# The first four weight units of three narrow stages read x before its norm, and the norm's factor is put on afterwards

## The reference, cut to what matters

```python
def rms_norm(x, g):
    y = xf * lax.rsqrt(jnp.mean(xf * xf, axis=-1, keepdims=True) + RMS_EPS)
    return (y * g.astype(jnp.float32)).astype(x.dtype)
def mod_norm(x, m, i, g):
    return rms_norm(x, g) * (1 + m[:, 3 * i + 1, None]) + m[:, 3 * i, None]
def swiglu(h, w1, w2):
    a, b = jnp.split(h @ w1, 2, axis=-1)
    return (jax.nn.silu(a) * b) @ w2
...
        h = mod_norm(x, m, 1, norm_g[l, 1])
        u = h @ w_in[l]
        if last:
            uc_kv = hc @ w_in[l][:, OFF_K:]
```

## Time and profile before

| | us |
|---|---|
| median of 3 executions | 2800.92 (2800.55 to 2805.89) |
| profiled execution, its own time | 2799.17 |
| span of the profiled execution | 2797.3 |
| TensorE busy | 2732.1 (98%) |
| VectorE busy | 2067.0 (74%) |

### The profile page before, as it was taken

One profiled execution on the slowest core, in us unless ns is written; L12 is line 12 of the kernel. 1 busy time (PEld: TensorE's weight loads), 2 busy tenths in 40 slices (PEclk: granted clock), 3 DMA queues, 4 the chain that ended last, 5 costly groups with the idle time before them and its releaser, 6 DMA issues.

```text
span 2797.3 us, 40204 instructions
## 1 busy us (share of the span) xinstructions
PE 2732.1 (98%) x15618; PEld 2320.2 (83%) x15618; DVE 2067.0 (74%) x3773; ACT 1216.9 (44%) x2228; POOL 522.2 (19%) x449
## 2 busy tenths in 40 slices
PE   7999999999999999999988999999999999999998
PEld 5888878668888878888885999889999888888887
DVE  6989895568989896564766766765896677777776
ACT  5323233453232342222445545565556444444444
POOL 1111114300111101010050000345898000000000
PEclk9999999999999999999999999999999999999999
DMA  7555533223555445354441566424654556655554
GB/s 290 194 186 192 185 136 112 76 103 123 202 182 190 175 154 189 122 191 145 146 148 45 191 216 216 146 84 151 197 152 121 185 190 192 192 193 190 190 190 132
DMA packets 123261, 462.50 MB, mean 165 GB/s; under 512 B 13504, under 2 KB 26688, under 8 KB 109888
## 3 DMA queue, kind: packets, MB, share of 16 engines
q1 hardware_dynamic: 109248, 359.27, 39.5%
q0 software_dynamic: 13824, 100.67, 9.3%
HBM read 452.93 MB, written 6.95 MB: 164 GB/s over the span
## 4 chain that ended last, share of the span: by engine, by line
PE 90%; DVE 7%; issue 1%; ACT 1%; DMA 1%; POOL 1%; POOLq 0%; DVEq 0%; ACTq 0%
PE bank L283 28%; PE bank L284 27%; PE bank L285 27%; PE bank L2469 2%; DVE weight_lo L182 1%; DVE extension_ffn L920 1%; DVE nmax L1397 1%; DMA extension_ffn<-in_w_mods 1%; DVE arena L544 1%; PE bank L940 1%; PE bank L941 1%; PE bank L385 0%; PE bank L508 0%; DVE extension_mixer L1390 0%; POOL weight_lo L235 0%
## 5 line engine op out<-in xcount | busy, mean ns | idle before, releaser
L175 ACT ACTIVATE weight_hi<-weight_ring 128x512 fp32r<-128x512 f32 x1272 | 798.7, 631 | 1188.2 <-PE bank L285 1187.1
L182 DVE TENSOR_TENSOR weight_lo<-weight_ring,weight_hi 128x512 fp32r<-128x512 f32 x1110 | 839.4, 760 | 430.6 <-ACT weight_hi L175 428.9
L283 PE MATMUL bank<-operand_hi,weight_hi 128*128 128x256 f32 (+1 forms) x3168 | 1045.4, 330 | 16.8 <-DVE operand_lo L561 5.6
L284 PE MATMUL bank<-operand_lo,weight_hi 128*128 128x256 f32 (+1 forms) x3168 | 1032.8, 326 | 0.0
L285 PE MATMUL bank<-operand_hi,weight_lo 128*128 128x256 f32 (+1 forms) x3168 | 1032.6, 326 | 0.0
L283 PEld LDWEIGHTS bank<-operand_hi,weight_hi 128*128 128x128 f32 x3168 | 602.2, 190 | 86.1 <-issue 16.1
L284 PEld LDWEIGHTS bank<-operand_lo,weight_hi 128*128 128x128 f32 x3168 | 602.6, 190 | 53.1 <-issue 0.5
L285 PEld LDWEIGHTS bank<-operand_hi,weight_lo 128*128 128x128 f32 x3168 | 602.1, 190 | 50.4
L920 DVE SCALAR_TENSOR_TENSOR extension_ffn<-extension_ffn,silu_c 128x512 f32<-128x512 f32 x532 | 388.4, 779 | 1.7
L235 POOL TENSOR_TENSOR weight_lo<-weight_ring,weight_hi 128x512 fp32r<-128x512 f32 x162 | 211.6, 1315 | 421.1 <-ACT weight_hi L175 418.3
L283 PE MATMUL bank<-hidden_hi_ffn,weight_hi 128*128 128x512 f32 (+1 forms) x704 | 256.6, 364 | 4.0 <-DVE arena L1173 4.0
(11 more groups left out here) (280 smaller groups left out, 2543.5 us busy)
## 6 DMA issues: line engine op xcount, KB each, us to landing
weight_ring<-in_ffn SPq DMA_DIRECT2D x272, 512.0 KB, 3.5
weight_ring<-in_experts SPq DMA_DIRECT2D x256, 512.0 KB, 3.5
extension_ffn<-in_w_mods POOLq DMA_DIRECT2D x96, 1024.0 KB, 7.6
weight_ring<-in_w_mix SPq DMA_DIRECT2D x56, 512.0 KB, 3.4
weight_ring<-in_w_second SPq DMA_DIRECT2D x52, 512.0 KB, 3.6
spill<-early_retrieve SPq DMA_DIRECT2D x45, 128.0 KB, 3.9
arena<-spill SPq DMA_DIRECT2D x45, 128.0 KB, 3.5
extension_mixer<-in_rel_bias SPq DMA_DIRECT2D x2, 1536.0 KB, 6.7
```

The lines of the kernel that those rows point to most:

```text
L175: nc.scalar.activation(self.hi[:, g % 2, h], self.ring[:, g % NS, h], ACT.Copy).then_inc(self.rounded, 1)
L182: self.nc.vector.tensor_tensor(self.lo[:, g % 2, h], self.ring[:, g % NS, h], self.hi[:, g % 2, h].bitcast(F32), ALU.subtract).then_inc(se ...
L283: nc.tensor.matmul(out, a_hi, b_hi, start=start and n == 0, stop=False)
L284: nc.tensor.matmul(out, a_hi, b_lo, start=False, stop=False)
```

## The change

In A, B and C the first four units don't read the normed operand. While the stage before finishes x tile by tile, ScalarE rounds x times gain (`round_raw`) and VectorE takes the rest (`split_raw`), into columns that are free then: the context half of the operands in A and B, the unused half of the hidden buffers in C. Two more columns hold the shift vector, so that each such matmul has 258 columns. TensorE starts the pair of units 0 and 1 at once, with `sums` behind kt 2 and `spread` behind kt 4, and goes on with units 2 and 3 on the same operand. When a bank is full, VectorE copies its shift column to a small tile and multiplies the 256 columns by the norm's factor, which `copy_rstd` has copied from bank 7 to memory, and ScalarE adds the shift (in B as the bias of silu, for value units VectorE adds it in `hide`). From unit 4 on the normed operand is used, whose scales, roundings and splits are made meanwhile, in an order written out in `late_scalar` and `late_vector`. All `keep_warm` of these three norms go.

In A the context columns are normed later (`SplitNorm`), two tiles in each of units 4 to 7, before the wide units that need them, and the masks of GpSimd wait for twelve evicted units in place of four. In C x2 is made in units 4 and 5 in place of 0 to 3.

```diff
+def late_pair(units, pe, outs, norm):
+    nc = units.nc
+    for kt in range(KT):
+        i = kt // (KT // 2)
+        if kt % (KT // 2) == 0:
+            w = [units.half(pe, 0, j, i) for j in range(2)]
+        pe.wait_ge(norm.raw_in.sem, norm.raw_in.at(kt + 2))
+        b = slice(kt * P - i * HALF, (kt + 1) * P - i * HALF)
+        for j in range(2):
+            last = product(nc, outs[j], [((w[j][0][:, b], w[j][1][:, b]), norm.raw_operand(kt))], start=(kt == 0), stop=(kt == KT - 1))
+            if j == 0 and kt % (KT // 2) == KT // 2 - 1:
+                last.then_inc(units.used, 1)
+        if kt == 2:
+            norm.sums(pe)
+        if kt == 4:
+            norm.spread(pe)
+    last.then_inc(units.used, 2)
...
+        pad = 2 if width > S else 0
+        hi, lo = (sb(f"operand_{part}", [P, KT, width + pad], F32R) for part in ("hi", "lo"))
+        self.hi, self.lo, self.raw = hi[:, :, 0:width], lo[:, :, 0:width], (hi[:, :, width - S:], lo[:, :, width - S:])
...
+    def raw_operand(self, kt):
+        return self.raw[0][:, kt, :], self.raw[1][:, kt, :]
+    def round_raw(self, act, kt):
+        nc, hi = self.chip.nc, self.raw[0]
+        if kt == 0:
+            nc.scalar.activation(hi[:, :, S:S + 2], self.columns, ACT.Copy).then_inc(self.raw_rounded.sem, 1)
+        nc.scalar.activation(hi[:, kt, 0:S], self.x[:, kt, 0:S], ACT.Copy, scale=self.gain(kt, 0)).then_inc(self.raw_rounded.sem, 1)
+    def split_raw(self, dve, kt):
+        nc, (hi, lo) = self.chip.nc, self.raw
+        if kt == 0:
+            dve.wait_ge(self.raw_rounded.sem, self.raw_rounded.at(1))
+            nc.vector.tensor_tensor(lo[:, :, S:S + 2], self.columns, hi[:, :, S:S + 2].bitcast(F32), ALU.subtract)\
+                .then_inc(self.raw_in.sem, 1)
+        dve.wait_ge(self.raw_rounded.sem, self.raw_rounded.at(kt + 2))
+        nc.vector.scalar_tensor_tensor(lo[:, kt, 0:S], self.x[:, kt, 0:S], self.gain(kt, 0), hi[:, kt, 0:S].bitcast(F32),
+                                       ALU.mult, ALU.subtract).then_inc(self.raw_in.sem, 1)
...
+    def copy_rstd(self, dve):
+        self.chip.nc.vector.tensor_copy(self.chip.rs[:, :], self.rstd(0, S)).then_inc(self.rs_there.sem, 1)
+        dve.wait_ge(self.rs_there.sem, self.rs_there.at(1))
...
+    def late_scalar(self, act, units, evict):
+        units.round(act, 0, 2, [0])
+        self.round_one(act, 0, 0)
+        self.round_one(act, 1, 0)
+        units.round(act, 0, 2, [1])
+        units.round(act, 0, 3, [0])
+        self.round_one(act, 2, 0)
+        evict(0)
+        self.round_one(act, 3, 0)
+        evict(1)
+        self.round_one(act, 4, 0)
+        units.round(act, 0, 3, [1])
+        self.round_one(act, 5, 0)
+        self.round_one(act, 6, 0)
+        units.round(act, 0, 4, [0])
+        self.round_one(act, 7, 0)
+        evict(2)
+        units.round(act, 0, 4, [1])
+        units.round(act, 0, 5, [0])
+        evict(3)
+        units.round(act, 0, 5, [1])
...
+    def late_vector(self, dve, units, evict, middle=None):
+        units.subtract(dve, 0, 2, [0])
+        self.scale(dve, 0, 0)
+        self.scale(dve, 1, 0)
+        self.split(dve, 0, 0)
+        self.scale(dve, 2, 0)
+        self.split(dve, 1, 0)
+        units.subtract(dve, 0, 2, [1])
+        units.subtract(dve, 0, 3, [0])
+        self.copy_rstd(dve)
+        evict(0)
+        self.scale(dve, 3, 0)
+        self.split(dve, 2, 0)
+        evict(1)
+        self.scale(dve, 4, 0)
+        self.split(dve, 3, 0)
+        if middle:
+            middle()
+        units.subtract(dve, 0, 3, [1])
+        self.scale(dve, 5, 0)
+        self.split(dve, 4, 0)
+        self.scale(dve, 6, 0)
+        self.split(dve, 5, 0)
+        self.scale(dve, 7, 0)
+        self.split(dve, 6, 0)
+        units.subtract(dve, 0, 4, [0])
+        self.split(dve, 7, 0)
+        evict(2)
+        units.subtract(dve, 0, 4, [1])
+        units.subtract(dve, 0, 5, [0])
+        evict(3)
+        units.subtract(dve, 0, 5, [1])
...
             if kt == 0 and not self.by_sums:
                 pe.wait_ge(self.gathered.sem, self.gathered.at(KT - 2))
             else:
-                if not self.by_sums:
+                if not self.by_sums and not self.raw:
                     c.keep_warm(pe, self.spare, 3)
                 pe.wait_ge(self.squared.sem, self.squared.at(kt + 1))
...
-        self.chip.keep_warm(pe, self.spare, 5)
...
-        c.keep_warm(pe, self.spare, 6)
...
-        c.keep_warm(pe, self.spare, 7)
...
+        if self.late:
+            pe.wait_ge(self.norm.after.sem, self.norm.after.at(self.norm.first + 6))
+            late_pair(units, pe, [chip.bank[j][:, 0:S + 2] for j in range(2)], self.norm)
+            for u in range(2, self.late):
+                units.chunk(pe, 0, u, chip.bank[u][:, 0:S + 2], self.norm.raw_operand)
...
+        def hide(n):
+            g, hi, lo = self.gate_buf[:, n, 0:S], self.hid_hi[:, n, 0:S], self.hid_lo[:, n, 0:S]
+            dve.wait_ge(self.silu_done.sem, self.silu_done.at(n + 1))
+            dve.wait_ge(self.scaled.sem, self.scaled.at(2 * n + 2))
+            nc.vector.scalar_tensor_tensor(g, self.tb, chip.late_bias[:, 2 * n + 1:2 * n + 2], g, ALU.add, ALU.mult)\
+                .then_inc(self.ffn_step.sem, 1)
+            dve.wait_ge(self.ffn_step.sem, self.ffn_step.at(2 * n + 1))
+            first, rest = split_activations(nc, hi, lo, g)
+            first.then_inc(self.ffn_step.sem, 1)
+            dve.wait_ge(self.ffn_step.sem, self.ffn_step.at(2 * n + 2))
+            rest().then_inc(self.gated.sem, 1)
+        def evict(n):
+            dve.wait_ge(units.used, units.used_at(n))
+            nc.vector.tensor_copy(chip.late_bias[:, n:n + 1], chip.bank[n][:, S:S + 1])
+            nc.vector.tensor_tensor(self.tb if n % 2 else self.gate_buf[:, n // 2, 0:S], chip.bank[n][:, 0:S], chip.rs[:, :],
+                                    ALU.mult).then_inc(self.scaled.sem, 1)
+            if n == 3:
+                hide(1)
+        if self.late:
...
-        pool.wait_ge(self.evicted.sem, self.evicted.at(4))
+        pool.wait_ge(self.evicted.sem, self.evicted.at(CH_K if self.last else 4))
...
+                if self.last and n == CH_K:
+                    pe.wait_ge(self.norm.context_in.sem, self.norm.context_in.at(KT))
...
+            if self.last and n < KT:
+                norm.scale(dve, 2 * n - KT, 1)
+                norm.scale(dve, 2 * n - KT + 1, 1)
+                norm.split(dve, 2 * n - KT, 1)
+                norm.split(dve, 2 * n - KT + 1, 1)
...
+        norm.late_vector(dve, units, scaled)
+        for j in range(4, 6):
             units.subtract(dve, 0, j + 2)
-            if j < 4:
-                norm.x2(dve, 2 * j)
-                norm.x2(dve, 2 * j + 1)
+            for kt in range(4 * (j - 4), 4 * (j - 3)):
+                norm.x2(dve, kt)
```

More of the change, by code:

```diff
@@ L1020, in take_for_ffn @@
 def take_for_ffn(chip, ctx, name):
-    part = ([P, max(HIDDEN), T2], F32R)
+    part = ([P, max(HIDDEN), T2 + 2], F32R)
     mod = ([P, 1024], F32R)
@@ L1038, in __init__ @@
         self.then, self.double, self.transfers = None, False, []
+        self.late = 4 if norm.raw else 0
+        if self.late:
+            self.scaled, self.halves_out = chip.late_scaled.take(4), chip.late_out.take(2)
+            self.tb = chip.part(A_RSTD + 512, S)
         beside = {None: (0, 0, 0), 12: (0, 0, 1), 16: (2, 2, 1)}[work.n if work else None]
@@ L1198, in __init__ @@
         self.mix = None
+        self.scaled = chip.late_scaled.take(4) if norm.raw else None
     def sync(self, sp):
@@ L1229, in tensor @@
         chip, nc, units, hi, lo = self.chip, self.chip.nc, self.units, self.hi, self.lo
-        self.norm.sums(pe)
-        self.norm.spread(pe)
+        late = self.norm.raw
+        if not late:
+            self.norm.sums(pe)
+            self.norm.spread(pe)
         for n in range(0, 16):
@@ L1256, in scalar, with evict @@
         self.norm.root(act)
-        self.norm.round(act)
-        for n in range(16):
+        late = 4 if self.norm.raw else 0
+        def evict(n):
+            act.wait_ge(self.scaled.sem, self.scaled.at(n + 1))
+            nc.scalar.activation(self.u[:, n, 0:S], self.u[:, n, 0:S], ACT.Identity, bias=chip.late_bias[:, n:n + 1])\
+                .then_inc(self.evicted.sem, 1)
+        if late:
+            self.norm.late_scalar(act, units, evict)
+        else:
+            self.norm.round(act)
+        for n in range(late, 16):
             units.round(act, 0, n + 2, [0])
@@ L1857, in out_half @@
             units.part_chunk(pe, 28 + a, i, add_out(bank, n), x, 1, n % 2 == 0 or n == 7, False, None if n else self.y_split)
-        norm.sums(pe)
-        norm.spread(pe)
-        units.pair(pe, [bank[0][:, 0:S], bank[6][:, 0:S]], x, norm.split_in)
-        for j in range(2, 8):
+        late_pair(units, pe, [bank[0][:, 0:S + 2], bank[6][:, 0:S + 2]], norm)
+        for j in range(2, 4):
+            units.chunk(pe, 0, j, bank[j - 1][:, 0:S + 2], norm.raw_operand)
```

(17 more changed lines are left out.)

152 lines of the change are left out of this document (122 added, 30 removed).

## The result

The changed kernel takes 2824.64 us (median of four runs, 2823.83 to 2828.26) against 2801.69 of the kernel before in the same comparison: ratio 1.0086, 95% interval 1.0074 to 1.0098. It is slower by 23 us, where I had forecast 5.5 faster. The profiled execution took 2823.83 us, with a span of 2822.0 against 2797.3.

A forecast was written before the change was run, and what follows sets the result against it. TensorE is busy 98%, so only its waits or useless work can be won; VectorE becomes the new bound at the norms. -7.6 + 0.9 + 1.2 = -5.5 us from 2800.92 gives 2795.4 us, range 2787 to 2803.

The forecast's parts named there:

- Wider matmuls: 258 instead of 256 columns in 96 matmuls a stage: between 0 and 1.1 us a stage, 0.1 by column count.
- the slower one: Rival: VectorE's chain from first scale to split 7 binds longer, 3 us more a stage, up to 2809.5 us; chance 0.11.
- The sum of the stages: Changes at the three norms added up: -7.6 + 0.9 + 1.2 = -5.5 us.
- A, -7.6: First of the three norms: unit 4 comes 6.0 us earlier, unit 12 at 1439.9 to 1440.0 against 1447.63, 7.6 us won.
- the masks, 3.9: Units 4 to 12 of the first norm's stage: moving GpSimd's masks later removes three weight_lo waits and restarts, 3.9 us won.
- B, +0.9: Second norm: unit 4 0.4 us earlier, then 1.1 of waiting and 0.2 for restarts and wider matmuls, 0.9 us lost.
- the last tile is ready some 2 us after T0 and is wanted 5 us after it: Raw operands fit into the units before each norm and cost nothing; uncovered they would cost up to 3.2 us a stage.
- C, +1.2: Third norm: unit 4 1.4 us earlier, then waits of 1.1 and 1.6, unit 6 at 1777.7 against 1776.46, 1.2 us lost.
- The waits: TensorE waits 1.8 us in unit 3, 1.5 before unit 4, 1.1 behind it, and 1.6 in unit 5 of the third stage.
- The rival of shorter waits: Rival: VectorE and ScalarE interlock better; up to 10.7 us better, 2784.7, half of that 2790; chance 0.20.
- the one on hand-offs: Part of the slower rival (0.11): each VectorE-ScalarE hand-off costs 0.35 us more, one way to lose 3 us more a stage.
- The clock: Rival: without keep_warm TensorE's waits lower the granted clock, 1.7 us a fall; one or two give 2797 to 2799; chance 0.14.

The follow-up runs named there:

- the tiles in place: Changed kernel with 512-word rows up to the first norm's stage and 32 unused words realigning the hidden tiles, against the kernel before: 2797.96 us, 0.9991.
- VectorE adding first: The late-rows, realigned version of the changed kernel, with VectorE adding the bank to x before raw split and gathering: 2797.56 us, 0.9984 to the kernel before.

## Why the prediction was wrong

**The step that failed is "Wider matmuls".** I priced the two columns as two columns: 96 narrow matmuls, 0 to 1.1 us a stage. That they lengthen the rows of tiles which every stage shares, and so move lo rows and hidden rows against the weights, I didn't look at. The diff shows it, in `Chip.take` and `take_for_ffn`, and no row of before could price it, as all its moving rows lay in place. The runs put 26 us (1.0094) there, against a total of 23. None of my rivals was of that kind; the slower one reached 2809.5 by VectorE's chain and had 0.11, with 0.08 for a slower kernel in all. The two columns themselves cost what I said: 120.4 ns of pitch against 119.8 for 256 columns, under 0.1 us a stage.

**The sum of the stages** was -5.5. With equal rows on both sides it is -3.4 by lags, and -2.7 by medians with the tiles in place (0.9991). Term by term:
- A, -7.6: the lag shrank by 8.1 from T0 to unit 12 in the changed kernel, and by 7.3 in the run of A alone with tiles in place, where TensorE stands 0.72 us for weight_lo ahead of the pair. Right, and the timetable too: unit 4 at 17.6 against 18.0.
- Of it the masks, 3.9: the masks alone won 3.9 by the lag, and 5.5 by the medians (2.2 to 7.3 by the interval). Right as a term. Wrong in what I took for granted, that masks and new order add up: the new order with early masks stands at 1.0004. That each slowed subtraction now hits a chain without slack is how I read it; the waits for weight_lo, 10.7 us against 3.8, fit. I had named VectorE as the new bound, and should have priced the masks against that bound.
- B, +0.9: +2.4, or +4.0 with the clock's fall, as in the changed kernel. The failed step is "the last tile is ready some 2 us after T0 and is wanted 5 us after it", which I took to show that the raw operands cost nothing in front. The tile was in time. The weights' half behind it wasn't: it waited in VectorE's queue, 1.83 us where 0.5 was to be had. With VectorE adding first B costs 1.1 and comes to unit 4 in 17.3 us, where I had said 17.0.
- C, +1.2: +1.7 in the changed kernel, +1.9 in the runs with the tiles in place. Right in its steps, but for 0.50 us that TensorE stands ahead of the pair, with unit 4 and unit 6 within 0.4 us.

**The waits.** 1.58, 1.29 and 0.88 us at A for my 1.8, 1.5 and 1.1; the same three at B and C, within 0.4 of those, and 1.4 for 1.6 in unit 5 of C. The rival of shorter waits had little in it, as had the one on hand-offs. **The clock** fell at B, behind the wait ahead of the pair, in four of five traces that have it (1.83 to 2.04 us), and never behind the waits that I had in mind, though that in unit 3 of B was as long: 1.93 to 1.98 us in seven traces. So the length of a wait alone doesn't decide it.

**What is the best version?** Stage A alone, late masks, tiles in place: 2791.81 us, 0.9970 (0.9960 to 0.9980), faster than both kernels. Against the kernel with the masks late alone (0.9983, 0.9974 to 0.9992) the intervals overlap; by lags its new order adds 3.4 us to the masks' 3.9. B loses 2.4 us, or 1.1 with VectorE adding first, and C 1.7 to 1.9, by lags: there the norm left too little to win for the work that VectorE gets in return.

Left open: why the pitch depends on 256 bytes between weights and moving rows. A conflict of the next weights' load with the reading of the moving operand would fit, but that is a guess: no run separates it from other causes. Nor is it known why the experts' matmuls, which take rows of the weights as moving operand, had some 230 ns in both kernels and not 227, though by the order of the tiles they too begin a multiple of 256 bytes from the weights.

## What to carry to other kernels

An edit that lengthens or shifts a tile is an edit of every instruction that reads it or anything allocated behind it. Compare addresses before pricing: here moving rows at other than a multiple of 256 bytes from the weights cost on average 5 to 6 ns in 227 on each wide matmul. If the loss is there before the code that was changed runs, plot the lag against the instruction's number: an even slope is a pitch, a step is a wait. And a cost found beside slack (the masks, 3.9 us) must be priced again when the change uses the slack up; it was 8 to 10 us then.

## What the runs showed of the hardware

- 128x512 matmuls in f32r: 226.8 to 226.9 ns of pitch with all moving rows 0 or 256 bytes (modulo 512) from the weights; with rows at other distances 231.7 to 232.7 on average, 228.7 to 235.9 by row; 27.5 us of 2800 for a shift of 128 bytes, nothing for 256. 128x256 matmuls on the operand weren't slower: 119.8 ns before, 119.3 off by 128.
- The same wait of 1.83 to 1.85 us ahead of B was followed by a granted clock of 0.50 and 0.54 in two traces and of 1.00 in a third, and waits of 1.93 to 1.98 us in unit 3 of B by no fall in seven. The 2.67 us wait of the convolution, 57 us ahead of B's, was followed by one in 13 of 17 traces. Which of the two places has a fall, or whether both have, differs between kernels that do the same work in other places of the memory.
